# Six of the conv mixer's 31 taps summed by GpSimd in a buffer of its own, which VectorE adds

## What is computed

```python
def conv_mixer(h, w_pw1, w_dw, b_dw, norm_g, w_pw2):
    u = h @ w_pw1
    u = u[..., :D_MODEL] * jax.nn.sigmoid(u[..., D_MODEL:])
    u = dwconv(u, w_dw) + b_dw
    u = jax.nn.silu(rmsnorm(u, norm_g))
    return u @ w_pw2
```

## Time and profile before

| | us |
|---|---|
| median of 3 runs | 1939.31 (1937.58 to 1940.23) |
| time of the profiled execution | 1940.57 |
| its span, first to last instruction | 1938.8 |
| TensorE busy | 1789.0 (92%) |
| VectorE busy | 1438.7 (74%) |
| ScalarE busy | 1050.4 (54%) |
| GpSimd busy | 48.3 (2%) |

### The profile page before, as it was taken

The page is one execution under the profiler, slowest core; times in us unless marked ns, Lnnn a source line. Parts: engine busy times, 40 slices in busy tenths (PEclk is TensorE's granted clock), DMA queues, the critical chain, the costliest instruction groups (busy, mean ns, idle before and its releaser), DMA issues.

```text
span 1938.8 us, 24560 instructions
## 1 busy us (share of the span) xinstructions
PE 1789.0 (92%) x8828; PEld 1465.3 (76%) x8828; DVE 1438.7 (74%) x1626; ACT 1050.4 (54%) x999; POOL 48.3 (2%) x95
## 2 busy tenths in 40 slices
PE   5899998799998975689999999999999999999993
PEld 1788786799997753468888888888888888888883
DVE  1434344565555796379999999999999999999995
ACT  1222224444332102167777777777777777777772
POOL 0011000000000000100000000000000000000001
PEclk7999999899999896789999999999999999999997
DMA  9366569444443562379999999999999999999972
GB/s 389 125 239 222 203 225 346 171 163 178 181 185 130 231 266 95 135 292 378 380 376 377 383 371 387 374 376 384 372 383 370 382 382 374 375 381 378 386 296 87
DMA packets 63000, 568.54 MB, mean 293 GB/s; under 512 B 7268, under 2 KB 7396, under 8 KB 15204
## 3 DMA queue, kind: packets, MB, share of 16 engines
q1 hardware_dynamic: 54144, 539.13, 72.0%
q0 software_dynamic: 5392, 19.41, 2.8%
q10 hardware_dynamic: 3412, 9.28, 1.2%
HBM read 549.43 MB, written 18.36 MB: 293 GB/s over the span
## 4 chain that ended last, share of the span: by engine, by line
PE 82%; DVE 10%; DMA 3%; issue 2%; ACT 2%; POOL 0%; DVEq 0%; POOLq 0%; SPq 0%; ACTq 0%
PE ps L1469 22%; PE ps L1471 22%; PE ps L1470 22%; PE ps L1340 5%; DVE work L1127 5%; PE ps L1337 3%; DMA ring<-mix 2%; PE ps L1462 1%; PE ps L1624 1%; DVE w_lo L1237 1%; PE ps L1276 1%; ACT w_hi L803 1%; PE ps L1387 1%; PE ps L1540 1%; PE ps L1357 1%
## 5 line engine op out<-in xcount | busy, mean ns | idle before, releaser
L1237 DVE TENSOR_TENSOR w_lo<-ring,w_hi 128x1536 fp32r<-128x1536 f32 x504 | 873.5, 1755 | 76.8 <-ACT w_hi L803 76.4
L803 ACT ACTIVATE w_hi<-ring 128x1536 fp32r<-128x1536 f32 x504 | 750.7, 1492 | 232.5 <-PE ps L1471 222.2
L1469 PE MATMUL ps<-w_hi,hg 128*128 128x512 f32 x1072 | 424.5, 396 | 6.7 <-DVE w_lo L1237 4.4
L1470 PE MATMUL ps<-w_lo,hg 128*128 128x512 f32 x1072 | 419.3, 391 | 0.0
L1471 PE MATMUL ps<-w_hi,hg 128*128 128x512 f32 x1008 | 393.6, 391 | 0.0
L1471 PE MATMUL ps<-w_hi,hid 128*128 128x512 f32 x680 | 265.6, 391 | 0.0
L1469 PE MATMUL ps<-w_hi,hid 128*128 128x512 f32 x616 | 242.0, 393 | 3.0 <-DVE hid L1231 3.0
L1470 PE MATMUL ps<-w_lo,hid 128*128 128x512 f32 x616 | 240.1, 390 | 0.0
L1469 PEld LDWEIGHTS ps<-w_hi,hg 128*128 128x128 f32 x1072 | 202.4, 189 | 47.5 <-DVE w_lo L1237 4.8
L1470 PEld LDWEIGHTS ps<-w_lo,hg 128*128 128x128 f32 x1072 | 202.6, 189 | 40.8
L1471 PEld LDWEIGHTS ps<-w_hi,hg 128*128 128x128 f32 x1008 | 189.8, 188 | 40.2
(11 more groups left out here) (227 smaller groups left out, 1638.4 us busy)
## 6 DMA issues: line engine op xcount, KB each, us to landing
ring<-moe SPq DMA_DIRECT2D x252, 1536.0 KB, 8.3
ring<-mix SPq DMA_DIRECT2D x92, 1024.0 KB, 6.7
ring<-ff SPq DMA_DIRECT2D x28, 1536.0 KB, 6.4
xg<-work POOLq DMA_DIRECT2D x12, 512.0 KB, 4.9
so<-xg POOLq DMA_DIRECT2D x10, 512.0 KB, 8.8
yg<-so ACTq DMA_DIRECT2D x10, 512.0 KB, 9.1
work<-c POOLq DMA_DIRECT2D x8, 257.0 KB, 7.2
c_out<-work ACTq DMA_DIRECT2D x8, 257.0 KB, 5.7
```

The source lines that it names most:

```text
L803: act.activation(w_hi[:, s % W_BUFS, :], ring[:, sl, s % 2 * CUT * ROW:(s % 2 + 1) * CUT * ROW], ACT.Copy).then_inc(hi_ready, 1)
L1237: TT(w_lo[:, s % W_BUFS, :], ring[:, slot(ST_MOE + s // 2), s % 2 * CUT * ROW:(s % 2 + 1) * CUT * ROW], w_hi[:, s % W_BUFS, :].bitcast(f32 ...
L1469: pe.matmul(out, a_hi, b_hi, start=start, stop=False)
L1470: pe.matmul(out, a_hi, b_lo, start=False, stop=False)
```

## The change

VectorE sums taps 0 to 24 as before. Taps 25 to 30 are GpSimd's: it multiplies tap 25 into `side`, and for each of the other five multiplies into `side_tap` and adds that to `side`, waiting for its own step each time through `side_step`. `side` has two buffers by the parity of s. VectorE waits for `side_ready`, adds `side` to the odd sum, waits for that in `link`, and adds the two sums as before.

```diff
+POOL_TAPS = 6
+OWN_TAPS = B_TAPS - POOL_TAPS
...
+        side = carve(2, T)
+        side_tap = carve(T)
...
             norm_root(2)
+            steps = 0
+            for s in range(N_PW1):
+                pool.wait_ge(glu_done, s + 1)
+                if s >= 2:
+                    pool.wait_ge(cv_ready, s - 1)
+                to = side[:, s % 2, :].rearrange("p (g t) -> p g t", g=G)
+                for t in range(OWN_TAPS, B_TAPS):
+                    w = vec[:, V_BCONV + t * KD + s:V_BCONV + t * KD + s + 1]
+                    src = pad31[:, s, :, t:t + P]
+                    if t == OWN_TAPS:
+                        pool.tensor_scalar(to, src, w, None, ALU.mult).then_inc(side_step, 1)
+                        steps += 1
+                        continue
+                    pool.tensor_scalar(side_tap.rearrange("p (g t) -> p g t", g=G), src, w, None, ALU.mult
+                                       ).then_inc(side_step, 1)
+                    steps += 1
+                    pool.wait_ge(side_step, steps)
+                    ins = pool.tensor_tensor(to, to, side_tap.rearrange("p (g t) -> p g t", g=G), ALU.add)
+                    if t < B_TAPS - 1:
+                        ins.then_inc(side_step, 1)
+                        steps += 1
+                        pool.wait_ge(side_step, steps)
+                ins.then_inc(side_ready, 1)
             norm_root(3)
...
-                for t in range(B_TAPS):
+                for t in range(OWN_TAPS):
...
-                n_chain[0] = begun + B_TAPS
+                n_chain[0] = begun + OWN_TAPS
                 dve.wait_ge(dve_chain, n_chain[0])
+                dve.wait_ge(side_ready, s + 1)
+                link(TT(even_odd[1], even_odd[1], side[:, s % 2, :].rearrange("p (g t) -> p g t", g=G), ALU.add))
                 TT(out, out, even_odd[1], ALU.add).then_inc(cv_ready, 1)
```

More of the change, by code:

```diff
@@ L343, in mlstm_conformer_kernel @@
                                                            sem("sq_ready"), sem("ssq_done"))
+        side_step, side_ready = sem("side_step"), sem("side_ready")
         rb_ready, z_ready, ez_ready, zs_ready = sem("rb_ready"), sem("z_ready"), sem("ez_ready"), sem("zs_ready")
```

## The result

| | before | after |
|---|---|---|
| median, us | 1939.77 (4 runs, 1937.58 to 1940.38) | 1953.76 (4 runs, 1951.44 to 1956.23) |
| ratio to before | 1 | 1.0074, 95% interval 1.0057 to 1.0092 |
| profiled execution: time, span, us | 1940.57, 1938.8 | 1951.44, 1949.7 |
| one turn of the conv loop, us | 13.31 | 14.92 |

What follows compares the result with a forecast made beforehand. VectorE's turn in the conv mixer was taken as the bound: 11.39 us of its own work plus 5.7 of GpSimd's gives 17.1, 3.8 longer, over eight groups 30.3 us; 1939.31 + 30.3 = 1969.6, predicted 1970, range 1923 to 1990.

Steps and rivals of the forecast that it cites:

- The bound: Conv mixer: VectorE's turn of 13.31 us a group sets the span, so any change to it counts eight times.
- VectorE's own work: Conv loop: six taps less (2.38 us), one addition more (0.46 us), turn from 13.31 to 11.39 us.
- GpSimd's prices: GpSimd's new instructions of 256 elements: multiplication 0.435 us, addition 0.618 us, estimated from memsets.
- The chain: GpSimd's 11 instructions a group with handoffs: 6.6 us, with 5.5 and 11.4 as ends.
- the spare time: GpSimd's 6.6 us chain fits the 9.8 us until VectorE's 25 taps are done, 3.2 us to spare.
- That the two engines disturb each other: Taps beside GpSimd's SBUF reads: they contend, between nothing and 5.7 us a turn; the upper end taken as judgement.
- How much: Conv loop: all GpSimd's 5.7 us added to VectorE's 11.39, turn 17.1 us, 3.8 us longer than before.
- My second rival: Taps beside GpSimd: only part of each instruction excludes; turn 14.8 us, 1951; lower part (1928 to 1943) chance 0.08.
- the cruder one: Taps beside GpSimd: whole instructions take turns, turn 17.1 us, 1970; whole or nearly so, chance 0.52.
- The page's rule: Two-input VectorE instructions contend with GpSimd's SBUF reads, not writes; the first holds the ports throughout; kernel becomes slower.
- starvation: Rival: GpSimd gets no turn during the taps and VectorE waits for its chain; turn 18.0 us, 1977, chance 0.14.
- The case on the other side: First rival: nothing shared, GpSimd's chain hidden, turn 11.39 us, time 1924.0, chance 0.24.

Runs made afterwards that it cites:

- the first experiment: Changed kernel with GpSimd's taps 25 to 30 left out, GpSimd only writing one element a group and signalling: 1923.14 us, ratio 0.9909 to the kernel before.

## Why the prediction was right and wrong

**The bound.** Right. The conv mixer runs at VectorE's turn, and the 1.61 us by which the turn grew appear eight times in the span.

**VectorE's own work.** Right: 11.39 us counted, 11.39 measured when GpSimd does nothing.

**GpSimd's prices.** Wrong. "A multiplication takes between 223 + 255 x 0.83 = 435 ns and 733 ns. I take 435": it takes 925, beyond even the upper end. The rate came from a memset, which reads nothing; the two-element difference of 2 ns an element, which I set aside as scatter, pointed nearer but still gave 0.19 too little. What sets a multiplication's length no run shows. The additions, 0.73 against my 0.62, were inside their bounds. The chain is 10.0 us, not 6.6, and the spare time, which I had at 3.2, is negative: with sums in PSUM VectorE waits for it. In the changed kernel itself this did no harm, since there the 23 taps take 12.6 us.

**That the two engines disturb each other.** Right, and now shown from four sides: without GpSimd's work, with writes only, and with one SBUF operand in the tap the taps lose nothing; with half the elements they lose about half.

**How much.** This is the step that failed: "the two take turns, and the whole of GpSimd's 6 x 0.435 + 5 x 0.618 = 5.7 us is added to VectorE's turn". Measured is 3.53 us. The engines do not take turns by instruction; a tap that starts just behind a GpSimd instruction of 256 elements loses 0.22 us to one with one operand and 0.48 to one with two, and the rest of each GpSimd instruction lies beside the taps. By its true durations, 6 x 0.925 + 5 x 0.726 = 9.2 us, full exclusion would have made the turn 20.6 us and the time near 1998; that my sum came out at 1970 is two errors that partly offset each other. My second rival, sharing in part with only the elements excluding, described the mechanism and gave 14.8 us and 1951 against 14.92 and 1953.8. I had it in the right form and gave the weight to the cruder one, by judgement and no row, with the page named below behind it. Its 3.4 us are the 16 operands that GpSimd reads in a group (6 multiplications with one, 5 additions with two), 256 elements each at the memset's 0.83 ns: 16 x 0.213 = 3.4. That number was partly luck: the same rate misses a multiplication's own length by half, and no run shows why it fits the hold.

**The page's rule.** The Trainium skill, "SBUF — State Buffer", section "Who interferes with whom": the first half of what the prediction cites from it, that a VectorE instruction with two SBUF inputs contends with a GpSimd one that reads SBUF, is what the runs show (3.5 us a turn lost with reads, none in the taps with writes, none with one operand in PSUM). The second half, that the first to come holds the shared ports for the whole instruction, stands for two SBUF inputs in the Trainium skill, "SBUF — State Buffer", section "SBUF: two separate sides". The runs don't bear it out: a GpSimd multiplication of 0.97 us holds a tap for 0.22, and a tap that starts 0.72 us into it not at all. The section "Who interferes with whom" of that page of the Trainium skill also says that VectorE's TENSOR_SCALARs can enter modes with both port pairs, in which VectorE contends with GpSimd. That fits the 0.20 us beside the memsets; no run shows which mode they were in.

**The other rivals.** No starvation: GpSimd's instructions beside the taps are at most 0.3 us longer than alone, most only 0.05 or not at all. No wait for `side_ready` in the turn. The case on the other side, nothing shared, is what the first experiment builds, at 1923.1 where 1924.0 was worked out.

## What to carry to other kernels

Work moved from VectorE to GpSimd need not be free for VectorE, even when it is hidden: count the SBUF operands GpSimd will read and set what they took from VectorE, here 0.22 us for 256 float32 and 0.48 for a pair, against the instruction saved, here 0.396. If VectorE's instruction can take one of its two operands from PSUM, try that: here the collision went away and the same move paid, 1930.8 us against 1953.8. When a stage is bound by one engine, try the idle ones together, and price each by a row of an instruction that does the same reads; a memset is no measure for a multiplication.

## What the hardware showed that I had not expected

- A one-input GpSimd multiplication of 128x256 float32 with a per-partition weight takes 0.925 us alone, longer than a two-input addition, 0.726 us (VectorE's TENSOR_SCALAR of this shape and kind: 0.35 to 0.41 us).
- VectorE's accumulating instruction with its sum in PSUM starts every 0.392 us, with it in SBUF every 0.396; a first TENSOR_SCALAR into PSUM takes 0.55 us against 0.41.
- GpSimd memsets beside VectorE's TENSOR_SCALARs stretch these from 0.41 and 0.35 to 0.48 and 0.47 us, and are themselves stretched once from 0.31 to 0.45.
- Behind a GpSimd multiplication a tap loses 0.22 us at 256 elements and 0.11 at 128, so no fixed part of it costs VectorE anything; more than three quarters of one lies beside the taps unnoticed (0.22 us lost to 0.97).
- The hold goes both ways: a multiplication that starts 0.03 us ahead of a tap leaves that tap alone, takes 1.21 us instead of 0.93, and the tap after it loses 0.14.
